# Retention products in three rounded passes, rings of two buffers, and stores issued by SyncE, in a decoder step on one core

## The reference, cut to the retention layer

```python
def body(S, xs):
    qc, kc, vc = xs
    scores = jnp.einsum('bihd,bjhd->bhij', qc, kc) * decay_mask[None]
    intra = jnp.einsum('bhij,bjhe->bihe', scores, vc)
    cross = jnp.einsum('bihd,bhde->bihe', qc * q_dec, S)
    S_new = S * chunk_dec + jnp.einsum('bjhd,bjhe->bhde', kc * k_dec, vc)
    return S_new, intra + cross
```

## Time and profile before

| | us |
|---|---|
| median of 3 runs | 1816.89 (1816.76 to 1819.88) |
| the profiled execution | 1818.06 |
| its span, first to last instruction | 1816.4 |
| PE busy in the span | 1768.9 (97%) |
| DVE, ACT, POOL busy | 969.6, 777.3, 266.6 |
| retention heads | from about 58 to 784 |

### The profile page before, as it was taken

How to read it: one execution, slowest core, us unless ns; L and a number is a source line. 1 busy time by engine, 2 the same in 40 slices (tenths; PEclk the granted TensorE clock), 3 DMA queues, 4 the chain that set the end, 5 groups by cost and what they waited for, 6 DMA issues and landing times. The chain is left out here.

```text
span 1816.4 us, 27405 instructions
## 1 busy us (share of the span) xinstructions
PE 1768.9 (97%) x9783; PEld 1393.8 (77%) x9783; DVE 969.6 (53%) x1868; ACT 777.3 (43%) x1683; POOL 266.6 (15%) x324
## 2 busy tenths in 40 slices
PE   5999999999999999999999999999999999999998
PEld 3778787878787878777788877888877777677677
DVE  4663535353535454453546555676615657777762
ACT  3742323232323232332344333343326667888720
POOL 2000000000000000000000012101113545555300
PEclk8999999999999999999999999999999999999999
DMA  9231312131312121366434578424355548796252
GB/s 337 87 96 60 96 59 95 60 95 59 95 60 89 66 84 70 126 215 188 141 80 143 187 216 273 138 80 136 107 154 131 126 110 244 191 241 184 92 191 93
DMA packets 153897, 240.60 MB, mean 132 GB/s; under 512 B 13288, under 2 KB 102176, under 8 KB 152769
## 3 DMA queue, kind: packets, MB, share of 16 engines
q1 hardware_dynamic: 136778, 179.69, 33.4%
q0 software_dynamic: 17024, 59.66, 9.2%
HBM read 177.91 MB, written 61.42 MB: 132 GB/s over the span
## 5 line engine op out<-in xcount | busy, mean ns | idle before, releaser
L488 PE MATMUL rt_acc<-rt_w_hi,rt_h_hi 128*128 128x512 f32 x504 | 203.5, 404 | 1.0 <-DVE rt_h_lo L1030 1.0
L490 PE MATMUL rt_acc<-rt_w_hi,rt_h_lo 128*128 128x512 f32 x504 | 197.3, 392 | 0.0
L489 PE MATMUL rt_acc<-rt_w_lo,rt_h_hi 128*128 128x512 f32 x504 | 196.7, 390 | 0.0
L1709 POOL TENSOR_TENSOR pa_take<-pa_take,pa_after_key 128x512 f32<-128x512 f32 (+2 forms) x152 | 152.8, 1008 | 149.6 <-DVE pa_after_key L2032 145.3
L1073 DVE TENSOR_TENSOR rt_by_cos<-rt_raw,rt_cos 128x256 f32<-128x256 f32 (+1 forms) x72 | 30.5, 424 | 243.7 <-ACT rt_raw L903 243.7
L914 ACT COPY rt_qk_t<-rt_tr 128x256 f32<-128x256 f32 (+1 forms) x72 | 26.0, 361 | 278.6 <-PE rt_tr L722 278.6
L2982 PE MATMUL kq_acc<-kq_w_hi,kq_h 128*128 128x512 f32 x320 | 128.7, 402 | 0.0
L2985 PE MATMUL kq_acc<-kq_w_hi,kq_h 128*128 128x512 f32 x320 | 125.2, 391 | 0.0
L2983 PE MATMUL kq_acc<-kq_w_lo,kq_h 128*128 128x512 f32 x320 | 124.9, 390 | 0.0
L1920 ACT ACTIVATE pa_keep<-z,pa_bias 128x128 f32<-128x128 f32 (+3 forms) x192 | 110.8, 598 | 4.9 <-PE z L1773 4.6
L1920 ACT ACTIVATE pa_take<-z,pa_bias 128x128 f32<-128x128 f32 (+3 forms) x192 | 111.0, 602 | 0.0
(11 more groups left out here) (407 smaller groups left out, 4036.4 us busy)
## 6 DMA issues: line engine op xcount, KB each, us to landing
ro_a_raw<-retained SPq DMA_DIRECT2D x14, 1024.0 KB, 6.0
rt_w_raw<-in_ret_w_in SPq DMA_DIRECT2D x16, 512.0 KB, 5.0
rt_w_raw<-in_ret_w_in SPq DMA_DIRECT2D x8, 1024.0 KB, 8.1
rt_old<-in_state_ret SPq DMA_DIRECT2D x8, 1024.0 KB, 5.8
rt_g_raw<-in_ret_w_in SPq DMA_DIRECT2D x8, 1024.0 KB, 5.3
out_st_sample<-rt_new POOLq DMA_DIRECT2D x8, 1024.0 KB, 7.9
k_cols<-kq_parts POOLq DMA_DIRECT2D x16, 512.0 KB, 4.0
kq_w_raw<-in_sb_w_in SPq DMA_DIRECT2D x4, 2048.0 KB, 10.6
```

The source lines that it names most:

```text
L488: nc.tensor.matmul(dst, h_hi[:, k, cols], w_hi[:, k, :], start=k == 0, stop=False)
L489: nc.tensor.matmul(dst, h_hi[:, k, cols], w_lo[:, k, :], start=False, stop=False)
L490: last = nc.tensor.matmul(dst, h_lo[:, k, cols], w_hi[:, k, :], start=False, stop=k == KD - 1)
L1709: nc.gpsimd.tensor_tensor(own, own, later, ALU.mult).then_inc(weighed, 1)
```

## The change

- The three products of `attend` on the prompt tiles are made from rounded operands in three fp32r passes each (high by high, high by low, low by high), 9 matmuls of 256 columns for 6 f32 instructions. The sample tile and the scores stay f32.
- ACT makes `v_hi` and `q_hi` by second copies out of PSUM, DVE makes `k_hi`, `probs_hi` and `state_hi` by repeating the last operation with an fp32r output, and POOL makes the five low parts by subtraction (`rest_of_...`). PE waits for five more semaphores in `attend`.
- DVE's `rotate` waits for a new semaphore `raw_taken`, given before `v_hi` is written; for the sample tile the second copy of v goes behind the scaling.
- R is 2; `probs` has one buffer, and `mask` waits for the `attend` before.
- The new sample states are written over `old`; SP issues all the stores, and the next old states are loaded when that store has landed. `state_free`, `new_free` and `o_free` are replaced by waits on the stores' own semaphores.

The diff, cut:

```diff
-        R = 3
+        R = 2
@@ sync
+            def store_states(h):
+                sp.wait_ge(state_ready, after(h, NPT - 1))
+                sp.dma_start(t_out["st_prompt"]..., state[:]).then_inc(state_stored, 16)
+                sp.wait_ge(new_ready, h + (CR + 1))
+                sp.dma_start(t_out["st_sample"]..., old[:]).then_inc(old_stored, 16)
+            with sp.Fori(0, H - 1) as h:
+                sp.wait_ge(projected, h * NT + (NT + CR))
+                w_of.load(sp, t_in, h + 1)
+                store_states(h)
+                load_ada(h + 1)
+                sp.wait_ge(old_stored, h * 16 + 16)
+                load_old(h + 1)
+                load_gates_of(h + 1)
+                sp.wait_ge(o_out, h * TURNS + 4)
+                store_kept(h, slice(SEQ, SEQ + NS))
+                sp.wait_ge(o_out, h * TURNS + (TURNS + 1))
+                store_kept(h, slice(0, SEQ))
+            sp.wait_ge(projected, H * NT + CR)
+            first.load(sp, next_loaded)
+            store_states(H - 1)
+            sp.wait_ge(o_stored, (H - 1) * 32)
@@ gpsimd
+            def rest_of_state(h, t):
+                pool.wait_ge(state_ready, after(h, t))
+                nc.gpsimd.tensor_tensor(state_lo[:], state[:], state_hi[:].bitcast(F32), ALU.subtract).then_inc(state_lo_s, 1)
+            (rest_of_probs, rest_of_q, rest_of_v, rest_of_k likewise)
+            with pool.Fori(0, H) as h:
+                for t in range(NPT + 3):
+                    if 0 <= t - 3 < NPT - 1: rest_of_state(h, t - 3)
+                    if 0 <= t - 2 < NPT: rest_of_probs(h, t - 2)
+                    if 0 < t - 1 < NPT: rest_of_q(h, t - 1)
+                    if t < NPT: rest_of_v(h, t); rest_of_k(h, t)
@@ tensor, attend, t < NPT
+                    pe.wait_ge(v_lo_s, ...); pe.wait_ge(probs_lo_s, ...)
+                    nc.tensor.matmul(into, probs_hi[:], v_hi[:, slot, :], start=True, stop=False)
+                    nc.tensor.matmul(into, probs_hi[:], v_lo[:, slot, :], start=False, stop=False)
+                    nc.tensor.matmul(into, probs_lo[:], v_hi[:, slot, :], start=False, stop=t == 0)
+                    (if t: wait q_lo_s, state_lo_s, and three passes of q and state)
+                    pe.wait_ge(k_lo_s, ...), then three passes of k and v into st
@@ scalar, take
                 act.wait_ge(attended, freed(h, t, R))
                 nc.scalar.copy(v[0:r, t % R, :], src[0:r, 2 * DK:QKV])
-                if t == NPT:
-                    nc.scalar.copy(v[NS:P, t % R, :], src[0:r, 2 * DK:QKV])
                 (two scalings into raw)
+                last.then_inc(raw_taken, 1)
+                if t == NPT:
+                    last = nc.scalar.copy(v[NS:P, t % R, :], src[0:r, 2 * DK:QKV])
+                else:
+                    last = nc.scalar.copy(v_hi[:, t % R, :], src[:, 2 * DK:QKV])
@@ scalar, turn_out
+                if 0 < t < NPT:
+                    last = nc.scalar.copy(q_hi[:, t % R, :], tr[:, 0, 0:P])
@@ vector
-                dve.wait_ge(taken, after(h, t))
+                dve.wait_ge(raw_taken, after(h, t))
+                if t < NPT:
+                    last = nc.vector.tensor_tensor(k_hi[:, t % R, :], by_cos[:, 1], by_sin[:, 1], ALU.add)
+                dve.wait_ge(attended, freed(h, t, 1))
+                if t < NPT:
+                    last = nc.vector.tensor_tensor(probs_hi[:], sc[:, 0, 0:P], table, ALU.mult)
+                    if t < NPT - 1:
+                        nc.vector.tensor_scalar(state_hi[:], state_sum[:], decay, None, ALU.mult)
-                    dve.wait_ge(new_free, h + 1)
-                        last = nc.vector.tensor_tensor(new[:, pair, :], ..., old[:, pair, :], ALU.add)
+                        last = nc.vector.tensor_tensor(old[:, pair, :], ..., old[:, pair, :], ALU.add)
```

More of the change, by code:

```diff
@@ L679, in _ @@
             nc.gpsimd.memset(q_diag[:], 0.0).then_inc(cleared, 1)
[L680 to L704, removed]
@@ L705, in _, with rest_of_probs, rest_of_q @@
-            store_states(H - 1)
+            def rest_of_state(h, t):
+                pool.wait_ge(state_ready, after(h, t))
+                nc.gpsimd.tensor_tensor(state_lo[:], state[:], state_hi[:].bitcast(F32), ALU.subtract).then_inc(state_lo_s, 1)
+            def rest_of_probs(h, t):
+                pool.wait_ge(masked, after(h, t))
+                nc.gpsimd.tensor_tensor(probs_lo[:], probs[:], probs_hi[:].bitcast(F32), ALU.subtract).then_inc(probs_lo_s, 1)
+            def rest_of_q(h, t):
+                pool.wait_ge(turned_out, after(h, t))
+                nc.gpsimd.tensor_tensor(q_lo[:, t % R, :], qk_t[:, t % R, 0, :], q_hi[:, t % R, :].bitcast(F32),
+                                        ALU.subtract).then_inc(q_lo_s, 1)
@@ new lines, in rest_of_v, with rest_of_k @@
+            def rest_of_v(h, t):
+                pool.wait_ge(taken, after(h, t))
+                nc.gpsimd.tensor_tensor(v_lo[:, t % R, :], v[:, t % R, :], v_hi[:, t % R, :].bitcast(F32), ALU.subtract).then_inc(v_lo_s, 1)
+            def rest_of_k(h, t):
+                pool.wait_ge(rotated, after(h, t))
+                nc.gpsimd.tensor_tensor(k_lo[:, t % R, :], rot[:, t % R, 1, :], k_hi[:, t % R, :].bitcast(F32),
+                                        ALU.subtract).then_inc(k_lo_s, 1)
@@ L734, in attend @@
             def attend(h, t):
-                r = rows(t)
+                r, slot, into = rows(t), t % R, out[0:rows(t), 0, 0:DV]
                 pe.wait_ge(masked, after(h, t))
@@ L1114, in update @@
                     join(h)
-                    dve.wait_ge(new_free, h + 1)
                     for n, src in enumerate((acc[:, 0], acc[:, 1], st[:, 0], tr[:, 0])):
                         pair = slice(2 * n, 2 * n + 2)
-                        last = nc.vector.tensor_tensor(new[:, pair, :], src.rearrange("p (b e) -> p b e", b=2),
+                        last = nc.vector.tensor_tensor(old[:, pair, :], src.rearrange("p (b e) -> p b e", b=2),
                                                        old[:, pair, :], ALU.add)
```

134 lines of the change are left out of this document (87 added, 47 removed).

## The result

The changed kernel took **1836.39 us** (median, 1835.13 to 1838.35), the kernel before 1817.87 beside it: ratio 1.0108, 95% interval 1.0096 to 1.012. It is 18.5 us slower (17.5 to 21.8 by the interval) where 9.4 us less had been forecast, and the time lies outside the range. The forecast sign was wrong.

A forecast was written before the change was run, and what follows sets the result against it. PE was taken as the bound, busy 90.00 of 90 us in a head. Products -13.5, sample tile +1.6 and head 0 +2.5 sum to -9.4 us, giving 1807.5 us against the median; range 1802.5 to 1818.5.

The forecast's parts named there:

- The products: Attends on prompt tiles: passes 0.12 us apart, a full attend from 1.30 to 1.08 us; 13.5 us less in all.
- The term for tile 0: Attend of tile 0 in each head: from 0.87 to 0.72 us, 8 x 0.145 us less.
- Rivals A and D: A: passes 0.108 us each, 1801.1 us, chance 0.08; D: PE out of issued work in attends, 1834 us, chance 0.10.
- Stores, states in place, the copies on ACT, the score's signal: SP's queue, ACT's added copies and the score's wait for q_hi: cost 0; last head's load bound 1 us.
- Tile 8's turn: Slot 9, turn waiting for DVE's rotate: 0.2 us more per head, 1.6 us in all; listed wait 0.3 to 0.5.
- rival C: POOL and DVE hinder each other in slot 9: up to 1.4 us a head, 11 in all, to 1818.5; chance 0.12.
- Extra work that stays beside PE: Added ACT, DVE and POOL work per slot, POOL at most 3.2 us of 7.2: cost 0 in slots 3 to 8.
- ready some 4 us ahead: POOL's low parts of state and probs, done some 4 us before the next slot's attend wants them.
- R = 2 ... Cost 0 in heads 1 to 7: Take of tile t waits for the attend of t-2, starting 1.47 us after the turn, 0.8 later; cost 0.
- The cover of 3 us: Rotated tile, wanted 7 us after the turn and ready after about 3; 3 us of cover left despite the later take.
- Head 0: Input's split later: 0.27 us in slot 1, 1.1 us waits in slots 4 and 6; 2.5 us more, bounds 0.5 to 4.
- Rival B: Score or POOL's parts in slots 9 and 10 late by about 0.1 us each: 1810.5 to 1813.5 us, chance 0.17.

The follow-up runs named there:

- gpsimd_beside: no_low_parts with GpSimd subtracting buffers of zeros of its own at the same points, nobody waiting for them; 1815.69 us, ratio 0.9997 to the kernel before.
- rings_of_three: Changed kernel with three buffers of v and of the halves of k and v, DVE's order unchanged; 1821.44 us, ratio 1.0034 to the kernel before.
- early_mask: Changed kernel with DVE's update and mask ahead of the rotation, GpSimd taking q, state and probs before v and k; 1820.89 us.
- no_low_parts_rings: no_low_parts with three buffers of v and the high parts of k and v; 1805.06 us, ratio 0.994 to the kernel before.
- f32_products_rings: Changed kernel with the old f32 products, no rounded copies or low parts, and three buffers of v and rotated pairs; 1816.59 us, ratio 1.0003.
- no_low_parts: Changed kernel with GpSimd idle, passes on low parts reading the high parts instead; 1807.85 us, ratio 0.9962 to the kernel before.
- low_parts_on_vector: Changed kernel with early_mask's order on DVE, all five low parts made by DVE, GpSimd idle; 1826.89 us, ratio 1.0062 to the kernel before.

## Why the prediction was wrong

By the times less before of the table, the 29.5 us between the best case (-11.0) and the changed kernel (+18.5) come in three steps: the ring of two by itself 2.7, GpSimd at work beside DVE 8.0, and PE's dependence on GpSimd's results 18.8. The second is measured with zeros (gpsimd_beside), so it is rather too small and the third too large. The steps aren't independent: the third buffer alone gives back 13.0 us (rings_of_three), the order of DVE and GpSimd 13.7 (early_mask), GpSimd's v 8.0, probs on DVE 8.8, each from the changed kernel.

- **The products: right.** Passes 0.12 us apart; a later head of no_low_parts_rings is 1.50 us shorter than before, where 7 x 0.22 + 0.145 = 1.69 was forecast. The term for tile 0 is what is missing: slot 3 is 6.79 us before and 6.82 without low parts. Rivals A and D are out; no `issue` entry stands before these passes in the changed kernel. The trace also stays with its 0.12 us and not with 109 ns; the formula behind that number stands in the Trainium skill, "TensorE: Matmul & The Clock Gate", "Back-to-back issue gap", as the gap of an isolated matmul.
- **Stores, states in place, the copies on ACT, the score's signal: right.** f32_products_rings is level with before. The score waits for nothing.
- **Tile 8's turn: the number right, by luck.** 0.41 us, eight times, forecast 0.3 to 0.5 from the added copies on DVE. But no_low_parts has all these copies, and PE's list there has no such wait. With GpSimd at work beside it one appears (gpsimd_beside):

```profile
PE rt_tr L779 <- DVE rt_rot L1151: 1.8, 8, 0.2
```

In the changed kernel tile 8's by_cos takes 778 ns where it took 417 (rows below). So a good part of this wait is rival C's. The term itself, 0.2 us a head, was nearly there: slot 9 of no_low_parts is 4.44 us, 0.14 more than before less a shorter attention (4.52 - 0.22).
- **"Extra work that stays beside PE": the failing step.** GpSimd's busy time was bounded (5 x 0.64 = 3.2 us a slot; measured 3.0 on average: 44.1, 40.7, 36.2, 26.0 and 22.5 us for v, probs, state, k and q in 56 slots), though three of the five took more than 0.64 each: 787, 727 and 738 ns on average for v, probs and state. What was wrong is "ready some 4 us ahead": in slot 8 of head 4 probs' low part is done at 481.40 (start 480.94, 0.46 us) and its reader starts at 481.74. State's low part hangs on the update and probs' on the mask, and both of these stand on DVE behind the rotation of a later tile. I followed the round only from the rotation to PE's turn, not to what is queued behind it on DVE.
- **"R = 2 ... Cost 0 in heads 1 to 7": the same step once more.** The take starts 1.58 us behind the turn (481.61 and 483.19 in the rows above), forecast 1.47. The cover of 3 us was measured for the rotated tile alone. For the mask and GpSimd's two operations behind it there was none in slot 9. As the cost of the ring by itself the 0 was nearly right: 0.06 us a head without GpSimd (no_low_parts_rings).
- **Head 0: sizes wrong.** The waits for h_lo were forecast well: 1.1 twice and 0.27 more, measured 1.07 twice and 1.23 for 1.0. Not seen were 2.12 and 1.43 us for probs' low part ahead of slots 4 and 6, where on DVE also the split of the input stands between rotation and mask, and 1.35 in slot 9; ahead of slot 4 the subtraction itself took 1.43 us, beside the split of the gates' weights. Head 0 came out 8.6 us longer, where the 2.5 of loss and tile 8's 0.2 less its own saving of 1.69 had given 1.0. Slot 9 of head 0 is as in the other heads.
- **Rival B: the right signal, the wrong size.** It named POOL's parts in slots 9 and 10 as late by about 0.1 us each. In slot 9 it is 1.35 us; in slot 10 there is no wait.
- **Rival C: its mechanism was right, its evidence wrong.** I gave it 0.12 because of the scans of the earlier trace rows. They don't stand for the rotation's products: DVE and GpSimd of the changed kernel, by line and shape from 140 to 780 us, are

```profile
L1138 DVE TENSOR_TENSOR rt_by_sin<-rt_raw,rt_sin 128x128 f32<-128x128 f32 x112 | 58.6, 562 | 0.0
...
L1213 DVE TENSOR_TENSOR rt_g_lo<-rt_g_raw,rt_g_hi 128x1024 fp32r<-128x1024 f32 x14 | 20.2, 1444 | 0.0
...
L1136 DVE TENSOR_TENSOR rt_by_cos<-rt_raw,rt_cos 64x256 f32<-64x256 f32 x7 | 5.4, 778 | 0.0
```

```profile
L732 POOL TENSOR_TENSOR rt_v_lo<-rt_v,rt_v_hi 128x256 fp32r<-128x256 f32 x56 | 44.1, 787 | 334.6 <-ACT rt_v_hi L964 334.6
L723 POOL TENSOR_TENSOR rt_probs_lo<-rt_probs,rt_probs_hi 128x128 fp32r<-128x128 f32 x56 | 40.7, 727 | 0.0
```

by_sin was 285 ns in the kernel before. Contention alone is 8 us by gpsimd_beside, within the 11 that C allowed, and as C had it mostly in slot 9 (8 x 0.78 us).

The trace of the kernel before had better evidence than the scans, and I overlooked it: in the attention layer DVE multiplies two SBUF tiles of 128 x 64 eight times. Three of them have no GpSimd operation beside them and take 0.21 to 0.23 us; the five others take 0.30 to 1.16 us, and each ends 0.07 to 0.09 us after the GpSimd operation beside it:

```profile
1571.33 0.87 POOL L1709 TENSOR_TENSOR pa_take<-pa_take,pa_after_key 128x384 f32<-128x384 f32 x1 [0.65 <-DVE pa_after_key L2032]
1571.34 0.93 DVE L2019 TENSOR_TENSOR pa_take<-pa_take,sa_hidden 128x64 f32<-128x64 f32 x1
...
1696.27 0.21 DVE L2019 TENSOR_TENSOR pa_take<-pa_take,sa_hidden 128x64 f32<-128x64 f32 x1
```

The rule of the Trainium skill, "GPSIMD Engine Reference", "Specifications", on DVE instructions with two SBUF inputs is borne out in this case, and should have weighed more than a row of another instruction.

What stays open: 2.4 of the 3.4 us behind the heads in the profile of the changed kernel, why `kq_xn` is late in some of the kernels and not in others, and what the order of DVE and that of GpSimd give by themselves.

## What to carry to other kernels

Follow a late signal not only to its reader but along the engine's own order: whatever is queued behind the waiting operation inherits the wait, and a slot that is long enough says nothing of the short one. Before handing small operations to GpSimd, list what VectorE does at that moment with two operands in SBUF, and keep GpSimd out of the last leg of any round: here the low part wanted soonest went to VectorE and the one with the most time moved away from the rotation, and that with a third buffer was worth 20.6 us.

## What the hardware showed

- DVE and POOL hinder each other by a lot on f32 tensor-tensor operations whose inputs are both in SBUF; where one of DVE's inputs is in PSUM these traces show nothing of it. by_sin's pair of 128 x 128 took 1.05 us for some 0.5, by_cos of 64 x 256 778 ns for 417, the split of 1024 columns 1444 for 1217, while DVE's mask on scores from PSUM kept its 0.28 us.
- How long it takes goes by the other engine's operation: in the kernel before, DVE's product of 64 columns took 0.93 us beside a GpSimd operation of 0.87, and 0.21 alone.
- It goes both ways: POOL's subtraction of 128 columns took 0.46 us alone and three times that beside DVE's split of 1024 columns, which is what slot 4 waits for. POOL's timeline, head 4 of the changed kernel:

```profile
452.19 1.43 POOL L723 TENSOR_TENSOR rt_probs_lo<-rt_probs,rt_probs_hi 128x128 fp32r<-128x128 f32 x1
```

- The same subtraction of 256 columns is 0.74 us on POOL and 0.42 on DVE (low_parts_on_vector), of 128 columns 0.46 and 0.29.
